# Third attention: branch counts folded into a bias table, a weight stream and the convolution's mean moved inside it, the last gate built beside the routing

## The chip, the cores and the metric

One core of a Trainium2 chip runs the whole program. The metric is the device time of one execution in microseconds (us); lower is better. The core has a matrix engine (TensorE, PE in the rows, with its weight loads as PEld), VectorE (DVE), ScalarE (ACT), GpSimd (POOL), and SyncE (SP), which issues most of the transfers from device memory. Each engine works through its own list of instructions in order, and they wait for each other on semaphores.

## The reference, cut to what matters

Three mixing layers and a mixture of experts run on 256 tokens of width 1024. The change lies in the third layer and in what follows it:

```python
# 8 heads, 256 tokens; three causal branches: (window 128, step 1), (512, 4), (2048, 16)
s = q k^T / 8 - slope_h * (t - t')         # one bias per head
out = sum_i e^{m_i} o_i / sum_i e^{m_i} l_i    # the branches are joined by their denominators
conv = silu(layer_norm_2(depthwise_conv(a * sigmoid(b)), ln_g, ln_b))    # 512 channels
x = x + gt1 * (concat([attn, conv]) @ w_out)
h2 = rms_norm(x, g_norm2) * (1 + sc2) + sh2
x = x + gt2 * hier_moe(h2, ...)            # 32 experts, 2 for each token, all in float32
# sh2, sc2, gt2: columns 3D to 6D of  silu(c) @ w_mod + b_mod  (w_mod is 1024 x 6144)
```

A key that lies in more than one branch counts once for each branch. So the joined result is one softmax in which each exponential is multiplied by the number of branches that hold the key (0 to 3).

## The kernel before

**Weights.** All weights come as pieces of 2 MB into `ring`, six slots of 16 KB in each partition. `PLAN` (from `chunk_plan()`) is the order of the pieces; a piece is loaded when the piece six places ahead of it is used up. `PLACE[stage][c]` is the place of piece c of a stage. After the plan SP loads the experts' weights, two experts (a pair) at a time, six pieces of 2 MB for a pair: two for gate, two for up, two for down (`load_pair`, line 583). For these there are nine slots: the ring's six, and the tiles `K`, `G` and `Q`.

**The modulation.** `w_mod_2` is multiplied with silu(c) in 12 pieces of 512 columns; columns 3D to 6D are the stage `mod_b`, six pieces (0 to 5). `stream(stage, c, bank)` on PE multiplies a piece and leaves a partial row (line 743; 738 for pieces 4 and 5, the gate gt2, whose rows are 512 wide), `mod_rows` on ACT copies the row out of PSUM (line 1340), and `fold` on PE turns it into columns (line 753). The gate is spread over all partitions by two products for each half (lines 1191 and 1192), and ACT copies it to `gate_row` (line 1533).

**The third attention** (`attention("c", ...)` on PE, ACT and DVE) has 8 units: 4 pairs of heads by 2 blocks of 128 queries (block 0 has 128 keys, block 1 has 256). For each unit: PE makes the scores of two heads (line 929), DVE adds the bias (`bias_c`, two instructions, line 1903) and takes the row maximum (line 1829), ACT takes the exponential (line 1387), DVE multiplies it by the branch counts and sums it (two instructions with an accumulator, line 1843), takes the reciprocal (1846) and scales (1850), PE turns the block (942), ACT copies it to `probT` (1404), PE multiplies with v (956), DVE copies the result out (1863). The engines run up to three units apart: in step n of its loop DVE does `take_out(n - 1)`, `row_max(n + 3)`, `sums(n + 2)`; PE turns unit n, makes the scores of unit n + 3 and multiplies unit n with v. The PE streams pieces 0, 1 and 2 of `mod_b` before unit 0.

**After it**, PE does in this order: `stream` of piece 3; the mean of the convolution over its channels (`feature_sum`, four products into bank 4); `stream` 4; `fold` 3; the mean of the squares (`feature_sum`, bank 2); `stream` 5; then `c_out`, the projection (`out_proj`, line 992, 8 output tiles of 8 products), which needs the attention's half of `mixT` at first and the convolution's half (from `nm["lnc", "out"]`) later. DVE subtracts the mean (2163), ACT squares (1415) and takes the root (1419), DVE takes the reciprocal (2166) and multiplies (2169), ACT applies silu (1516). Then come the logits (line 1146), the turned rows (1156), the routing on DVE (2219 to 2246), its ranks on PE (1198 to 1200), the choice of the first pair's tokens on DVE (2272), `gather` on PE (1212), and 16 pairs of experts (`experts`, gate and up at line 1246, down at 1278, the next pair's gather at 1212, the scatter at 1224). At the end of the second layer ACT issues five small loads (lines 1465 to 1471) just before it copies the rows of `mod_a`.

Of the kernel before, what the change touches and what calls it, by code (L numbers as in the profile page):

```python
# [18 lines left out]
ALU = mybir.AluOpType  # L19
# [31 lines left out]
def const_layout():  # L51
    at, n = {}, 0
    for name, w in (("ident", P), ("fold", 3), ("eps", 2), ("mean", P), ("before", P), ("dist", 2 * S),
                    ("mult", 2 * S), ("col", GRID_W), ("slot", CAP), ("desc", NE),
                    ("cos", S), ("sin", S), ("rot", P), ("band", 2 * P)):
        at[name] = (n, n + w)
        n += w
    return at, n


def constants():
    at, n = const_layout()
    out = np.zeros((P, n), np.float32)
# [25 lines left out]
    put("dist", np.where(mult > 0, d, BIG))  # L89
    put("mult", mult)  # L90
# [20 lines left out]
def chunk_plan():  # L111

    plan = []
    for stage, src, l, columns in (
# [8 lines left out]
            ("mod_b", "w_mod_2", 0, range(6, 12)), ("c_out", "w_out_2", 0, range(2))):  # L123
# [104 lines left out]
def build(nc, IN, consts_dram, relpad, out):  # L228
    CA, CN = const_layout()
    with ExitStack() as ctx:  # L230
# [40 lines left out]
        def vc(name, j=0):  # L271
# [64 lines left out]
                       "mod_b": U[:, 2048:3584].rearrange("p (b n) -> p b n", b=3)}  # L336
# [5 lines left out]
        def modrow(stage, c):  # L342

            if c < EARLY.get(stage, 0):
                return rows_beside[stage][:, c, 0:P]
# [13 lines left out]
        gate_row = cst[:, CA["dist"][0]:CA["dist"][0] + D]  # L359
# [8 lines left out]
        TURN = (6, 7, 4, 3)  # L368

# [92 lines left out]
        late_tables = cst[:, CA["dist"][0]:CA["mult"][1]]  # L462
# [73 lines left out]
        def _(sp):  # L536
# [16 lines left out]
            for n, (stage, src, l, c) in enumerate(PLAN):  # L553
                if n - SLOTS == PLACE["b_in"][5]:
                    sp.wait_ge(st["b_in"], used["b_in"][5])
                    load_bias(range(4))
                    sp.dma_start(late_tables, consts_dram[:, CA["dist"][0]:CA["mult"][1]]).then_inc(table_in, 16)
# [12 lines left out]
                if n == 5:  # L570
                    sp.dma_start(flat[:, 0:CN - CR], consts_dram[:, CR:CN]).then_inc(table_in, 16)
                    for c0, c1 in ((CF, CA["dist"][0]), (CA["mult"][1], CR)):
# [19 lines left out]
            load_pair(0, 0, after_plan, parts=range(4))  # L592
# [7 lines left out]
            load_pair(0, 0, after_plan, parts=(4, 5))  # L600
# [96 lines left out]
        def _(pe):  # L697
# [221 lines left out]
            def attention(L, q_of, k_of, v_of, stage, v0, nv):  # L919
# [18 lines left out]
                for n, (p, kind, qb, kts) in enumerate(un):  # L938
# [20 lines left out]
                    last.then_inc(at["pv"], 1)  # L959

# [22 lines left out]
            def out_proj(stage, src, width, late=KT, after=None):  # L983
# [13 lines left out]
                if late < KT:  # L997
                    for m in range(4):
                        part(m, range(late))
                    pe.wait_ge(nm["lnc", "out"], 4)  # L1000
# [7 lines left out]
            def feature_sum(bank, mat, src, n, width, ready, done):  # L1008

                for j in range(n):  # L1010
                    pe.wait_ge(ready, j + 1)
                    last = mm(ps[:, bank, 0:width], mat, src[:, j, 0:width], start=(j == 0), stop=(j == n - 1))
# [112 lines left out]
            pe.wait_ge(mod_ok, 6)  # L1125
            attention("c", lambda h, kind, qb: qTc[half(h), h // 2, qb * P:(qb + 1) * P],
# [1259 lines left out]
```

## Time and profile before

| | us |
|---|---|
| median of 3 runs | 1213.71 |
| lowest and highest | 1211.02, 1214.12 |
| the profiled execution, its own time | 1209.34 |
| the profiled execution, its span | 1207.3 |
| PE busy | 1152.9 (95%) |
| DVE busy | 544.6 (45%) |
| ACT busy | 295.7 (24%) |
| first expert product | 740.76 |

The span is the time from the first to the last recorded instruction. Busy time is what an engine's records cover. PEclk is the TensorE clock that was granted, as a share of full speed. The DMA share is the mean busy share of the core's 16 transfer engines. Times of rows are counted from the start of the span.

### The profile page before, as it was taken

How to read it: one execution, taken by the hardware profiler on the slowest of the kernel's cores; microseconds unless marked ns; L12 is line 12 of the kernel's file. 1: busy time of each engine (PE TensorE's matmuls, PEld its weight loads, DVE VectorE, ACT ScalarE, POOL GpSimd, SP SyncE). 2: the span in 40 equal slices, each digit the busy share in tenths (PEclk: the TensorE clock that was granted, in tenths of full speed). 3: DMA queues.
4: the chain of work that ended last, by engine and by line, in shares of the span. 5: the costliest groups of instructions: out<-in, count | busy, mean ns of one | idle time of the engine just before them, and what ended most of it. 6: DMA issues, size and time to landing. Idle time of an engine off the chain costs nothing.

```text
span 1207.3 us, 17553 instructions
## 1 busy us (share of the span) xinstructions
PE 1152.9 (95%) x7148; PEld 743.0 (62%) x7148; DVE 544.6 (45%) x1278; ACT 295.7 (24%) x705; POOL 22.7 (2%) x33
## 2 busy tenths in 40 slices
PE   4999999989999999999998998999999999999996
PEld 3486876668778888668885585444444444444442
DVE  3353339986575430872799623122222222222223
ACT  0000128850340001660612413111111111111112
POOL 0000000000000001110000000000000000000000
PEclk9999999999999999999999798999999999999999
DMA  9852128023442226566376695999999999999990
GB/s 344 318 209 73 68 93 326 1 75 136 140 178 101 70 70 183 124 188 211 140 279 228 246 301 202 428 427 428 426 429 428 427 429 429 427 428 430 427 413 39
DMA packets 82335, 311.54 MB, mean 258 GB/s; under 512 B 18130, under 2 KB 19229, under 8 KB 69467
## 3 DMA queue, kind: packets, MB, share of 16 engines
q1 hardware_dynamic: 78672, 309.56, 65.9%
q10 hardware_dynamic: 3386, 0.86, 0.3%
q8 instruction: 48, 0.79, 0.3%
q0 software_dynamic: 208, 0.17, 0.1%
q14 instruction: 21, 0.16, 0.0%
HBM read 309.40 MB, written 1.18 MB: 257 GB/s over the span
## 4 chain that ended last, share of the span: by engine, by line
PE 81%; DVE 12%; ACT 2%; DMA 2%; issue 1%; SPq 1%; ACTq 0%; DVEq 0%
PE ps L1246 18%; PE ps L891 17%; PE ps L1278 9%; PE ps L1212 5%; PE ps L992 5%; PE ps L1224 5%; DVE G L2146 4%; PE ps L956 2%; PE ps L942 2%; PE ps L840 2%; PE ps L1096 2%; PE ps L1072 2%; PE ps L929 2%; PE ps L743 2%; DMA ring<-in_a_w_in 2%; DVE soft L1824 1%
## 5 line engine op out<-in xcount | busy, mean ns | idle before, releaser
L1246 PE MATMUL ps<-ring,prob 128*64 128x512 f32 x704 | 188.1, 593 | 1.2 <-issue 1.2
L1246 PEld LDWEIGHTS ps<-ring,prob 128*64 128x64 f32 x704 | 61.9, 137 | 100.3 <-issue 100.3
L2311 DVE TENSOR_TENSOR prob<-ps,prob 128x512 f32<-128x512 f32 x16 | 17.2, 1075 | 193.7 <-PE ps L1246 193.7
L1278 PE MATMUL ps<-ring,prob 128*64 128x512 f32 x352 | 78.0, 596 | 0.0
L891 PE MATMUL ps<-U,ring 128*128 128x256 f32 x304 | 69.9, 381 | 1.6 <-DVE Q L1991 1.3
L1246 PE MATMUL ps<-K,prob 128*64 128x512 f32 x160 | 70.3, 592 | 0.0
L1212 PEld LDWEIGHTS ps<-bias,U 128*128 128x128 f32 x512 | 60.5, 198 | 13.4 <-issue 13.4
L1387 ACT ACTIVATE prob<-ps,soft 128x512 f32<-128x512 f32 (+2 forms) x112 | 64.1, 591 | 11.0 <-DVE soft L1829 9.0
L2319 DVE TENSOR_TENSOR probT<-ps,cst 128x512 f32<-128x512 f32 x32 | 22.1, 691 | 94.6 <-PE ps L1278 94.6
L1212 PE MATMUL ps<-bias,U 128*128 128x128 f32 x512 | 63.5, 284 | 1.1 <-DVE bias L2272 1.1
L891 PEld LDWEIGHTS ps<-U,ring 128*128 128x128 f32 x304 | 57.6, 190 | 9.9 <-DVE Q L1991 1.7
L1224 PE MATMUL ps<-probT,bias 128*128 128x512 f32 x128 | 57.9, 594 | 0.0
L1551 ACT ACTIVATE prob<-ps 128x512 f32<-128x512 f32 x16 | 9.6, 597 | 192.4 <-PE ps L1246 192.4
L1404 ACT ACTIVATE probT<-ps 128x512 f32<-128x512 f32 (+1 forms) x88 | 48.2, 585 | 34.4 <-PE ps L942 33.6
L992 PE MATMUL ps<-U,ring 128*128 128x256 f32 x256 | 56.4, 381 | 0.0
L1544 ACT ACTIVATE prob<-ps,H 128x128 f32<-128x128 f32 x64 | 24.0, 456 | 128.3 <-PE ps L1212 128.3
L942 PE MATMUL ps<-cst,prob 128*128 128x128 f32 x344 | 51.6, 288 | 2.4 <-DVE prob L1850 2.4
L992 PEld LDWEIGHTS ps<-U,ring 128*128 128x128 f32 x256 | 48.4, 190 | 7.1 <-issue 0.8
L1278 PEld LDWEIGHTS ps<-ring,prob 128*64 128x64 f32 x352 | 24.3, 137 | 45.8 <-issue 45.8
L929 PE MATMUL ps<-K,Q 64*128 64x512 f32 (+1 forms) x192 | 46.9, 568 | 1.9 <-ACT G L1375 1.3
L2296 DVE TENSOR_TENSOR U<-ps,U 128x512 f32<-128x512 f32 x64 | 44.2, 691 | 8.9 <-PE ps L1224 8.9
L2146 DVE SCALAR_TENSOR_TENSOR G<-G,conv_taps 128x256 f32<-128x256 f32 x120 | 47.7, 478 | 0.0
(378 smaller groups left out, 1839.2 us busy)
## 6 DMA issues: line engine op xcount, KB each, us to landing
ring<-in_w_exp_gate SPq DMA_DIRECT2D x22, 2048.0 KB, 18.2
ring<-in_w_exp_up SPq DMA_DIRECT2D x20, 2048.0 KB, 16.7
ring<-in_w_exp_down SPq DMA_DIRECT2D x20, 2048.0 KB, 19.9
ring<-in_w_ada SPq DMA_DIRECT2D x12, 2048.0 KB, 16.4
ring<-in_w_mod SPq DMA_DIRECT2D x12, 2048.0 KB, 8.8
ring<-in_b_w_in SPq DMA_DIRECT2D x8, 2048.0 KB, 9.0
ring<-in_a_w_in SPq DMA_DIRECT2D x5, 2048.0 KB, 17.7
ring<-in_w_in SPq DMA_DIRECT2D x5, 2048.0 KB, 9.2
```

The lines of the kernel that those rows point to most:

```text
L891: last = mm(ps[:, bank, 0:256], still[:, k, f * P:(f + 1) * P], moving[:, k, :], start=(k == 0), stop=(k == 3))
L929: last = mm(ps[:, 2 * (n % 2) + x, 0:len(kts) * P], q_of(h, kind, qb), k_of(h, kts), start=True, stop=True)
L942: last = tr(ps[:, 4 + i // 2, (i % 2) * S + x * P:(i % 2) * S + (x + 1) * P], prob[:, n % AHEAD, x * T + i * P:x * T + (i + 1) * P], ident)
L992: last = mm(ps[:, m % 4, 0:width], slot(n)[:, k, (m % 4) * P:(m % 4 + 1) * P], src[:, k, 0:width], start=(k == 0), stop=(k == KT - 1))
L1212: last = mm(ps[:, j // 4, (j % 4) * P:(j % 4 + 1) * P], h2rows[:, t, j * P:(j + 1) * P], pick[:, t, :], start=(t == 0), stop=(t == 1))
L1224: mm(ps[:, ACC_BANK[i], :], wpickT[:, t * P:(t + 1) * P], yrows[:, c * 512:(c + 1) * 512], start=True, stop=True).then_inc(scat, 1)
L1246: last = mm(ps[x * CAP:(x + 1) * CAP, 2 + i, :], xg[:, k, x * CAP:(x + 1) * CAP], chunk(n, 2 * i + x, turn)[0][:, k, :], start=(k == 0), s ...
L1278: last = mm(ps[x * CAP:(x + 1) * CAP, 5 + c, :], hidT[:, k, x * CAP:(x + 1) * CAP], chunk(n, 4 + x, turn)[0][:, k, c * 512:(c + 1) * 512], ...
L1387: last = a(prob[:, n % AHEAD, x * T:x * T + w], ps[:, 2 * (n % 2) + x, 0:w], ACT.Exp, bias=s[:, 1, x:x + 1], accum_out=None if L == "c" el ...
L1404: a(probT[:, i * S:i * S + w], ps[:, 4 + i // 2, 0:w], ACT.Copy).then_inc(at["copied"], 1)
L2146: ins = v.scalar_tensor_tensor(convo[:, j, :], glu[:, j, k:k + S], conv_taps[:, j, k:k + 1], convo[:, j, :], ALU.mult, ALU.add)
L2296: v.tensor_tensor(y, ps[:, b, :], y, ALU.add).then_inc(acc_ok, 1)
```

## The change

- Branch counts: the tables `dist` and `mult` go. A table for each head holds `log(count) - slope * distance`, or -1e30 where no branch has the key. `bias_c` adds it to both heads' scores in one instruction. ACT's exponential now makes the sum itself, and DVE's multiplication by counts goes. The table is 1.5 MB (`alibi`, in `Q`) and is loaded from ACT's queue, ahead of its copy of the row of `mod_a` piece 5; the 0.5 MB of `dist` and `mult` on SP's queue are no longer loaded.
- `mod_b` piece 3 is streamed after unit 1 of the attention. After unit 3, once DVE has taken unit 2 out, PE folds it and makes the convolution's mean (bank 5). DVE subtracts it (`center_conv`) after `sums(7)`.
- After the attention PE starts `c_out` at once; the mean of the squares is made after its first part.
- Pieces 4 and 5 are streamed after the last turned rows; `c_out` changes places with them in `PLAN`, and the loads of the first pair's up and down weights change places with them too. The gate's first half is spread after the ranks and before the first gather, its second half between the first gather and the totals.
- The load of the gate's bias row (`brow`, 4 KB) moves from the end of the attention to the five small loads of the second layer, as a sixth.
- DVE's preparation of the router's weights (`gains`, `wsum`) moves ahead of the convolution's reciprocal.

```diff
             ("c_in", "w_in_2", 0, (4, 3, 0, 1, 2)),
-            ("mod_b", "w_mod_2", 0, range(6, 12)), ("c_out", "w_out_2", 0, range(2))):
+            ("mod_b", "w_mod_2", 0, range(6, 10)), ("c_out", "w_out_2", 0, range(2)),
+            ("mod_b", "w_mod_2", 0, (10, 11))):
...
-                    sp.dma_start(late_tables, consts_dram[:, CA["dist"][0]:CA["mult"][1]]).then_inc(table_in, 16)
...
-            load_pair(0, 0, after_plan, parts=range(4))
+            load_pair(0, 0, after_plan, parts=range(2))
...
-            load_pair(0, 0, after_plan, parts=(4, 5))
+            load_pair(0, 0, after_plan, parts=range(2, 6))
...
                     last.then_inc(at["pv"], 1)
+                    if beside_unit:
+                        beside_unit(n)
...
+            def beside_c_unit(n):
+
+                if n == 1:
+                    stream("mod_b", 3, 5)
+                if n == 3:
+                    pe.wait_ge(at["o"], past["c", "o"] + 3)
+                    fold("mod_b", 3, 2, 1, 6)
+                    feature_sum(conv_mean, meanm, convo, 4, conv_ok, nm["lnc", "mean"])
+
+            def conv_variance(m):
+
+                if m == 0:
+                    feature_sum(ps[:, 5, 0:S], meanm, csq, 4, nm["lnc", "sq"], nm["lnc", "var"])
...
-            pe.wait_ge(at["o"], past["c", "o"] + len(UN["c"]) - 1)
-            stream("mod_b", 3, 5)
-            pe.wait_ge(conv_ok, 4)
-            feature_sum(4, meanm, convo, 4, S, conv_ok, nm["lnc", "mean"])
-            stream("mod_b", 4, 3)
-            pe.wait_ge(mod_ok, 7)
-            fold("mod_b", 3, 2, 1, 6)
-            feature_sum(2, meanm, csq, 4, S, nm["lnc", "sq"], nm["lnc", "var"])
-            stream("mod_b", 5, 5)
...
-            pe.wait_ge(nm["lnc", "std"], 1)
...
             turn_h(3)
-            for i, c in enumerate((4, 5)):
+            stream("mod_b", 4, 0)
+            stream("mod_b", 5, 1)
+
+            def spread_gate(i):
+
+                c = 4 + i
                 pe.wait_ge(row_ok, CHUNKS["mod_b"] + c + 1)
-                mm(ps[:, 1 + i, :], foldw, modrow("mod_b", c), start=True, stop=False)
...
             mm(ps[:, 5, NE:2 * NE], ones, sel[:, 0, :], start=False, stop=True).then_inc(ranks, 1)
+            spread_gate(0)
...
                 gather(r * PAIRS)
                 if r == 0:
+                    pe.wait_ge(h_row, 1)
+                    spread_gate(1)
                     totals()
...
                         last = a(prob[:, n % AHEAD, x * T:x * T + w], ps[:, 2 * (n % 2) + x, 0:w], ACT.Exp,
-                                 bias=s[:, 1, x:x + 1], accum_out=None if L == "c" else s[:, 2, x:x + 1])
+                                 bias=s[:, 1, x:x + 1], accum_out=s[:, 2, x:x + 1])
...
+                    if L == "c" and n == 3:
+                        mod_rows(stage, (3,), (5,))
...
+            act.dma_start(brow, IN["b_mod_2"][0:1, 5 * D:6 * D]).then_inc(rt_in, 16)
             mod_rows("mod_a", range(2, 4), (4, 5))
...
+            act.wait_ge(sig_ok, 4)
+            act.dma_start(alibi, consts_dram[:, CN:CN + NH2 // 2 * ALIBI]).then_inc(table_in, 16)
             mod_rows("mod_a", (5,), (6,))
...
-                    if L == "c":
-                        qb = un[n][2]
-                        mult = cs("mult")[:, qb * S:qb * S + w]
-                        for x in range(2):
-                            pr = prob[:, n % AHEAD, x * T:x * T + w]
-                            step(v.scalar_tensor_tensor(pr, pr, 1.0, mult, ALU.mult, ALU.mult,
-                                                        accum_out=s[:, 2, x:x + 1]))
-                        settle()
...
+                    if L == "c" and n + 3 == len(un):
+                        center_conv()
                 take_out(len(un) - 1)
+
+            def center_conv():
+                dve.wait_ge(nm["lnc", "mean"], 1)
+                dve.wait_ge(conv_ok, 4)
+                for j in range(4):
+                    v.scalar_tensor_tensor(convo[:, j, :], conv_mean, -float(D // HID), convo[:, j, :], ALU.mult, ALU.add
+                                           ).then_inc(nm["lnc", "cent"], 1)
...
-                for x in range(2):
-                    slope = 2.0 ** (-8.0 * (2 * p + x + 1) / NH2)
-                    sc = ps[:, 2 * (n % 2) + x, 0:w]
-                    step(v.scalar_tensor_tensor(sc, cs("dist")[:, qb * S:qb * S + w], -slope, sc,
-                                                ALU.mult, ALU.add))
+                sc = ps[:, 2 * (n % 2):2 * (n % 2) + 2, 0:w]
+                term = alibi[:, p * ALIBI + qb * 2 * P:p * ALIBI + qb * 2 * P + 2 * w].rearrange("p (x k) -> p x k", x=2)
+                step(v.tensor_tensor(sc, sc, term, ALU.add))
                 settle()
```

On ACT the copies of the rows of pieces 4 and 5 now stand after the turned rows and around the routing's first exponential, `take_gate(0)` after the four copies to `yacc`, and `take_gate(1)` after the first `take_gather`. The dummy root that fetches ACT's table for the convolution's root stands right after the squares.

## Rows read from the trace of the kernel before

**Rows 1.** Busy time by stretch, TensorE clock, DMA share and GB/s.

```profile
core 0: us, PE busy (x) PEld busy (x) DVE busy (x) ACT busy (x) POOL busy (x), PEclk, DMA share, GB/s
...
680.30:691.30 11.00, 11.00 (x116) 6.76 (x115) 3.35 (x8) 3.94 (x8) 0.00 (x0) 0.87 0.63 230
...
767.00:1181.00 414.00, 414.00 (x2054) 180.07 (x2050) 102.98 (x185) 60.40 (x112) 0.00 (x0) 1.00 1.00 423
```

**Rows 2.** The chain that ended last, from the third attention to the projection.

```profile
658.81 0.43 DVE prob L1843 x4
...
660.81 0.70 DVE prob L1843 x4
...
680.32 3.25 PE ps L743 x64
683.57 1.93 PE ps L1012 x8
...
691.35 17.47 PE ps L992 x80
```

**Rows 3.** The same view as rows 1, for three short stretches.

```profile
662.70:672.80 10.10, 10.05 (x52) 5.63 (x50) 9.69 (x43) 4.45 (x12) 0.00 (x0) 0.50 1.03 406
676.40:683.00 6.60, 5.61 (x68) 4.35 (x72) 1.54 (x7) 0.63 (x2) 0.00 (x0) 0.50 0.00 1
731.00:737.60 6.60, 5.50 (x26) 5.40 (x26) 0.84 (x3) 1.99 (x6) 0.00 (x0) 0.50 0.49 209
```

**Rows 4.** PE in order of time: start, duration, line, operands.

```profile
605.84 1.95 PE L743 MATMUL ps<-ring,sil 128*32 128x128 f32 x64
...
660.37 0.70 PE L929 MATMUL ps<-K 64*128 64x256 f32 x4
...
687.27 0.39 PE L753 MATMUL ps<-cst,prob 128*128 128x4 f32 x2
...
725.63 1.02 PE L1191 MATMUL ps<-prob,H 128*128 128x512 f32 x2
...
733.25 5.93 PE L1212 MATMUL ps<-bias,U 128*128 128x128 f32 x32 [1.09 <-DVE bias L2272]
...
739.17 0.39 PE L1205 MATMUL ps<-probT,H 128*128 128x32 f32 x2
740.76 13.95 PE L1246 MATMUL ps<-ring,prob 128*64 128x512 f32 x64 [1.21 <-issue]
754.65 3.84 PE L1212 MATMUL ps<-bias,U 128*128 128x128 f32 x32
```

**Rows 5.** DVE in order of time, convolution's normalisation.

```profile
690.17 1.75 DVE L2166 RECIPROCAL prob<-prob 128x256 f32<-128x256 f32 x1 [2.75 <-ACT prob L1419]
691.96 1.43 DVE L2169 TENSOR_TENSOR G<-G,prob 128x256 f32<-128x256 f32 x4
```

**Rows 6.** ACT and its queue in order of time, after the attention.

```profile
680.68 0.25 ACTq L1508 DMA_DIRECT2D cst<-in_b_mod  x1
...
686.45 1.42 ACT L1415 ACTIVATE G<-G 128x256 f32<-128x256 f32 x4 [2.53 <-DVE G L2163]
...
689.67 0.47 ACT L1419 ACTIVATE prob<-ps,cst 128x256 f32<-128x256 f32 x1
...
693.33 2.07 ACT L1516 ACTIVATE U<-G,vec 128x256 f32<-128x256 f32 x4
```

**Rows 7.** All engines in order of time, at the second layer's end.

```profile
540.82 2.17 ACTq L1470 DMA_DIRECT2D bias<-in_b_router_group  x1
...
543.30 1.56 ACTq L1471 DMA_DIRECT2D bias<-in_b_router_expert  x1
544.90 0.45 ACT L1340 ACTIVATE prob<-ps 128x128 f32<-128x128 f32 x2 [4.63 <-PE ps L743]
```

**Rows 8.** SP's issues late in the expert stage, in order of time.

```profile
1117.47 0.33 SPq L583 DMA_DIRECT2D K<-in_w_exp_up  x1
```

**Rows 9.** The same issue: size, and us from issue to landing.

```profile
K<-in_w_exp_up SPq DMA_DIRECT2D x1, 2048.0 KB, 21.7
```

**Rows 10.** PE's first product that reads that piece.

```profile
1145.87 0.59 PE L1246 MATMUL ps<-K,prob 128*64 128x512 f32 x1
```

More of the change, by code:

```diff
@@ L52, in const_layout @@
     at, n = {}, 0
-    for name, w in (("ident", P), ("fold", 3), ("eps", 2), ("mean", P), ("before", P), ("dist", 2 * S),
-                    ("mult", 2 * S), ("col", GRID_W), ("slot", CAP), ("desc", NE),
+    for name, w in (("ident", P), ("fold", 3), ("eps", 2), ("mean", P), ("before", P), ("late", D),
+                    ("col", GRID_W), ("slot", CAP), ("desc", NE),
                     ("cos", S), ("sin", S), ("rot", P), ("band", 2 * P)):
@@ L88, in constants @@
     mult = np.where(d >= 0, (d <= 128) * 1.0 + (d % 4 == 0) + (d % 16 == 0), 0.0)
-    put("dist", np.where(mult > 0, d, BIG))
-    put("mult", mult)
+    for h in range(NH2):
+        slope = 2.0 ** (-8.0 * (h + 1) / NH2)
+        term = np.where(mult > 0, np.log(np.maximum(mult, 1.0)) - slope * d, -BIG)
+        for qb in range(2):
+            w = (qb + 1) * P
+            c0 = n + h // 2 * ALIBI + qb * 2 * P + h % 2 * w
+            out[:, c0:c0 + w] = term[:, qb, 0:w]
     qc, kc = np.arange(P)[:, None] % GRID_W, np.arange(GRID_W)[None, :]
@@ L981, in _, with out_proj @@
             attention("a", q_a, k_a, v_a, "ada1", 0, 2)
-            def out_proj(stage, src, width, late=KT, after=None):
+            def out_proj(stage, src, width, late=KT, between=None, after=None):
                 def part(m, ks):
@@ L1173, in beside_c @@
                     token_logits(m - 2)
-            out_proj("c_out", mixT, S, late=4, after=beside_c)
+            out_proj("c_out", mixT, S, late=4, between=conv_variance, after=beside_c)
             token_logits(KT - 2)
@@ L1336, in mod_rows @@
                     act.wait_ge(st[stage], c + 1)
-                    if c >= 2 + EARLY.get(stage, 0):
+                    if 2 + EARLY.get(stage, 0) <= c and not spread(stage, c):
                         act.wait_ge(col_done, CHUNKS[stage] + c - 1)
@@ L2179, in _ @@
                 settle()
+            dve.wait_ge(nm["lnc", "std"], 1)
+            step(v.reciprocal(rstd[:, 0:S], rstd[:, 0:S]))
+            settle()
+            for j in range(4):
+                v.tensor_tensor(convo[:, j, :], convo[:, j, :], rstd[:, 0:S], ALU.mult).then_inc(acc2_ok, 1)
             for k in range(KT):
```

70 lines of the change are left out of this document (33 added, 37 removed).

## The prediction

> **What bounds the kernel now.** I read the view by stretch first [rows 1]. In the expert stage, from 767 us on, PE is busy without a gap (414.00 of 414.00 us) at full clock, so that whatever brings the first expert product (740.76) forward brings the end forward, as long as the weights follow. The DMA share there is also 1.00, a warning that is taken up below. Next comes the chain of work that ended last [rows 2]: through the third attention it runs over DVE (the counts' multiplication, line 1843, is on it), then over PE alone from 680.32: a stream, a feature sum, and so on to `c_out` at 691.35. In that stretch PE has no idle time at all [rows 1]. [...] So the change is worth what it moves the first expert product, and this sum is made from 656.5, where the attention starts, to 740.76.
>
> **The attention.** DVE loses line 1843 in all 8 units: 0.43 us on the chain for a unit with 128 keys, 0.70 for one with 256 [rows 2], so 4 x 1.13 = 4.5 us. The two bias instructions become one over the same elements; 0.02 us a unit at best, 0.2 in all. ACT gets an accumulator for each exponential: the nearest row is no row of this stage, so I bound it between 0 and 0.2 us an exponential; two for each unit, and DVE puts a `row_max` of about 1 us between the exponential and its use, which hides it. Without that cover it would be on the path with up to 0.4 x 8 = 3.2 us.
>
> What is added: after unit 1 PE has 1.95 us more (stream 3 at full clock [rows 4]). PE is only some 0.5 us ahead of what DVE wants next (the scores of unit 5, which stand behind the stream and the turning of unit 2), so about 1.4 us of it become a wait of DVE. After unit 3 come the fold, 0.39 [rows 4], and the mean, 1.93 [rows 2], together 2.3; behind them stand the turning of unit 4 and the scores of unit 7 (0.70 [rows 4]). Of this another 1.4 to 1.5 us reach DVE, since it still has `row_max(6)` and `sums(5)` (1.6 us) to do. `center_conv`, 4 instructions of the size of line 2169 (1.43 [rows 5]), delays `take_out(5)`, and PE's last product with v waits for that: 1.5 us more on DVE, of which about 0.9 shows at the end, as the end of the attention had waits of its own. Balance: -4.7 + 1.4 + 1.45 + 0.9 = -0.95; and the slow stretch cost the old attention about 1.0 us beyond DVE's work. So at full clock PE ends it at 680.3 - 2.0 = 678.3 and `c_out` starts at 678.5 after the last copy.
>
> **From there to the ranks.** `c_out` started at 691.35 [rows 2], now 678.5: -12.85 us. Into it comes the mean of the squares, 1.83 to 1.93: +1.85. Is the convolution ready in time? Squares follow the centering, 1.42 us [rows 6], done at 678.7, before PE has finished the first part (8 products' records of 0.218, that is 17.47/80 [rows 2]: 1.75 us). The sum ends at 682.1; root 0.47, reciprocal 1.75, first product 0.4, then four silu in 2.07 [rows 5, 6]: 686.9 with hand-offs. PE reaches the second halves at 682.1 + 3 x 1.75 = 687.4. So no wait, but with only half a microsecond to spare. The 8 instructions for the router's weights that now stand ahead of the reciprocal on DVE need about 2.5 us after 678.4 and end before the root. Streams 4 and 5 (under 2 us each) take the place of the four spread products in the shadow of DVE's routing: nothing. If that cover were gone they would cost 3.8.
>
> **Beside the first gather.** The first half of the gate (1.02 [rows 4] for one product, two products, 2.1 us) stands between the ranks and the gather, which waited 1.09 us for DVE [rows 4]: +1.0. The second half, 2.1 us, stands between the gather and the first expert product, where PE idled 1.21 [rows 4]: +0.9. The old gather lost 5.93 - 3.84 = 2.1 to the clock: -2.1 if it now runs at full clock.
>
> **The second layer.** ACT's last small loads already stand on the path: the copy of the rows follows the fifth directly, at 544.90 [rows 7]. A sixth costs 0.25 us by the same load in a quiet queue [rows 6] or up to 2.17 by its neighbours there [rows 7]. It is a single row of 4 KB, not 128 small ones, so nearer the low end: +0.6. [...] The issue of the 1.5 MB table stands ahead of ACT's copy of piece 5's row, for which ACT waits anyway until PE's stream that begins at 605.84 is over [rows 4], and the table is wanted at 656.5: nothing. Without this cover it would cost an issue, 0.25 to 2.17 again.
>
> **Sum at full clock**: -12.85 + 1.85 + 1.0 + 0.9 - 2.1 + 0.6 = -10.6 us.
>
> **The clock.** All this work is denser than before, and a slow stretch on it costs half its length, where in the old attention it was mostly hidden behind DVE. The old stretches were 10.2, 6.7 and 6.7 us long. I take one of the shorter kind on packed work: +3.4. So -7.2 us: span 1200.1, the profiled execution 1202.1, and from the median of the runs, 1213.71, which is 4.4 above the profiled execution: 1206.5.
>
> **Do the weights follow?** In the expert stage they land at 423 GB/s [rows 1], less than PE would eat, so that the lead shrinks. Late in it a piece is issued at 1117.47 and lands 21.7 us later, at 1139.2 [rows 8, 9]. PE's first record that reads it is at 1145.87 [rows 10]. The lead is 6.7 us. The stream's pace starts with the first slots that experts free, and so moves forward with PE. The last four pieces for the nine slots are now issued from the end of `c_out` on; at 2.1 MB and 423 GB/s that is 5.0 us a piece, 20 us. `c_out` ends 3 to 4 us before the spread products of 725.63 [rows 4], and the first slot was freed at half of 13.95 us after 740.76 [rows 4], 25 us after the end of `c_out`. So they are done about 5 us before. So the lead stays.
>
> **Rivals.** (A) As above, a slow stretch or two on packed work: gain 3.6 to 9.5 us, chance 0.60. (B) The clock stays full from 656 on: gain 10.6, 1203.1 us; denser work speaks for it, the lull of the routing against it. Chance 0.15. [...] (C) The work is hosted, but nothing is won: PE's queue is in order, and each thing put into the attention delays the scores DVE waits for. With slow stretches there as long as before (17 us, all now on packed work, +8.5) the gain is 2.1, 1211.6 us. Chance 0.18. (D) Slower: the slow clock holds through attention, first parts of `c_out` and both halves of the gate. Each microsecond costs 0.5; from 21 us on the gain is gone, from 28 us on it is slower by over 3.6 us; at 30 us it would be 1218. The 23.3 us of before show that such a sum is near, the dense `c_out` without any slow record speaks against it. Chance 0.07. (E) The weight stream does not move with PE: then 6.7 us is the most that can be won, 1207.0; this falls into A's figures.
>
> Changes within 0.3% (3.6 us) can't be told from none here. Faster by more: A and B, 0.75; within: C, 0.18; slower: D, 0.07. The range leaves out half of B's lower side and D: 1202.0 to 1212.5.
>
> **What would show it.** In the new profile: no multiplication with an accumulator on DVE in the attention; two waits of DVE on the scores of units 5 and 7 of 1 to 2 us each; the attention's end near 678 to 682; `c_out` directly behind, without a wait for the convolution; the first gather 1 us after its choice is made; the first expert product at 730 to 737; the expert stage still without PE idle and 466 us long. The prediction is wrong if PE waits for silu inside `c_out`, if the waits in the attention are 3 us and more, or if the first pair's up or down weights are late.

## The result, and the profile after

| | before | after |
|---|---|---|
| median, us | 1212.74 (4 runs) | 1198.82 (4 runs) |
| lowest and highest | 1211.02, 1214.12 | 1197.44, 1200.00 |
| the profiled execution: own time, span | 1209.34, 1207.3 | 1197.66, 1195.8 |
| first expert product | 740.76 | 731.75 |
| end of the last scatter product | 1196.5 | 1187.5 |

The ratio is 0.9892 [0.9879, 0.9905]: faster by 13.9 us at the medians, where the prediction said 7.2, and below its range, which ended at 1202.0. The first expert product came 9.0 us forward. From it to the last scatter product both kernels take the same 455.8 us. The rest of the gain lies behind the experts (2.5 us) and in the difference between a profiled execution and a median one: between the two profiled executions the gain is 11.7 us.

The chain that ended last, from the attention to the first gather of after, answers to [rows 2]:

```profile
663.76 1.89 PE ps L755 x64
665.64 0.37 PE ps L954 x2
666.01 0.63 PE ps L941 x4
...
669.35 1.83 PE ps L1027 x8
671.40 0.66 PE ps L941 x4
672.08 0.71 DVE ps L1938
...
677.17 0.67 PE ps L968 x8
678.21 1.99 PE ps L1006 x8
680.20 1.73 PE ps L1027 x8
681.93 15.62 PE ps L1006 x72
```

The hosted stream (L755) and the convolution's mean (the first L1027) are now on the chain, each with the scores of a later unit behind it (L941), and DVE adds the bias to these (L1938). `c_out` (L1006) starts at 678.21 directly behind the last product with v. The mean of the squares (the second L1027) stands after its first part, and then 72 products run as one: no wait for silu.

DVE of after in order of time, the two scores that it waits for:

```profile
666.69 0.70 DVE L1938 TENSOR_TENSOR ps<-ps,Q 128x512 f32<-128x512 f32 x1 [1.68 <-PE ps L941]
...
672.08 0.70 DVE L1938 TENSOR_TENSOR ps<-ps,Q 128x512 f32<-128x512 f32 x1 [1.46 <-PE ps L941]
```

PE of after in order of time, from the ranks to the first expert product, as in [rows 4]:

```profile
719.50 0.41 PE L1221 MATMUL ps<-probT,cst 128*128 128x32 f32 x2 [1.40 <-DVE probT L2269]
...
720.19 1.75 PE L1214 MATMUL ps<-prob,H 128*128 128x512 f32 x2
721.86 2.07 PE L1215 MATMUL ps<-cst,H 1*128 1x512 f32 x2
723.87 5.48 PE L1236 MATMUL ps<-bias,U 128*128 128x128 f32 x32
729.18 1.02 PE L1214 MATMUL ps<-prob,H 128*128 128x512 f32 x2
730.14 1.12 PE L1215 MATMUL ps<-cst,H 1*128 1x512 f32 x2
...
731.75 2.80 PE L1270 MATMUL ps<-ring,prob 128*64 128x512 f32 x12
```

Both halves of the gate (L1214, L1215) fill what had been two waits of PE. The first half took 3.8 us and the gather 5.48, the second half 2.1: only the first two ran at the slow clock. (At full clock the same gather takes 3.84, in `unhosted` below.) The view by stretch has the columns of [rows 1]; its first line answers to [rows 3], its second to [rows 1]:

```profile
720.50:727.30 6.80, 6.80 (x20) 3.93 (x19) 0.74 (x3) 1.19 (x4) 0.00 (x0) 0.50 0.99 410
762.00:1176.00 414.00, 414.00 (x2048) 180.42 (x2045) 105.40 (x185) 61.07 (x113) 0.00 (x0) 1.00 0.99 419
```

That is the only slow stretch between 600 us and the end of the experts; before had three there, 23.3 us together. (Both kernels also end at the slow clock, 5.3 and 4.3 us long, when PE has no work left.) PE is again without a gap through the expert stage.

**The tail.** The chain's last part, which the prediction does not mention. Before, and then after:

```profile
1197.47 0.07 DVEq L2341
1197.54 3.08 issue
1200.61 0.02 DVEq L2347
```

```profile
1188.46 0.06 DVEq L2365
1188.53 0.54 issue
1189.07 0.02 DVEq L2371
```

DVEq L2341 (L2365 in after) is DVE's branch past the further passes over the experts, which no execution here needs. From it to its next instruction DVE took 3.1 us before and 0.6 after: 2.5 us of the gain, in a place that no part of the change touches. "issue" in these rows is time in which the engine waited for nothing that the profile shows.

### The profile page after: what moved, and what is told of

Same layout as the page of the kernel before. It is cut to its first block, busy times and chain, and to the rows that moved or that the text cites. A ratio compares the mean times of both kernels' runs of the same rounds, so it can differ in the third digit from the quotient of the medians.

```text
span 1195.8 us, 17528 instructions
## 1 busy us (share of the span) xinstructions
PE 1145.7 (96%) x7148; PEld 735.3 (61%) x7148; DVE 540.7 (45%) x1236; ACT 297.2 (25%) x722; POOL 22.8 (2%) x33
## 4 chain that ended last, share of the span: by engine, by line
PE 83%; DVE 12%; DMA 2%; ACT 2%; issue 1%; SPq 1%; DVEq 0%; ACTq 0%
PE ps L1270 18%; PE ps L903 17%; PE ps L1303 9%; PE ps L1236 5%; PE ps L1006 5%; PE ps L1248 5%; DVE G L2180 4%; PE ps L968 2%; PE ps L941 2%; PE ps L852 2%; PE ps L1111 2%; PE ps L1087 2%; PE ps L954 2%; PE ps L755 2%; DMA ring<-in_a_w_in 2%; DVE soft L1859 1%
## 5 line engine op out<-in xcount | busy, mean ns | idle before, releaser
L1006 PE MATMUL ps<-U,ring 128*128 128x256 f32 x256 | 56.7, 381 | 0.4 <-DVE U L1890 0.4
L1006 PEld LDWEIGHTS ps<-U,ring 128*128 128x128 f32 x256 | 48.2, 190 | 7.1 <-DVE U L1890 0.6
L941 PE MATMUL ps<-K,Q 64*128 64x512 f32 (+1 forms) x192 | 46.8, 568 | 1.9 <-ACT G L1402 1.3
```

The costliest lines, as they stand in the source:

```text
L941: last = mm(ps[:, 2 * (n % 2) + x, 0:len(kts) * P], q_of(h, kind, qb), k_of(h, kts), start=True, stop=True)
L1006: last = mm(ps[:, m % 4, 0:width], slot(n)[:, k, (m % 4) * P:(m % 4 + 1) * P], src[:, k, 0:width], start=(k == 0), stop=(k == KT - 1))
```

## The experiments

Three questions were open: which part of the change brings the 9.0 us; whether the 2.5 us of the tail come with one of its parts, or only from where the branch stands in DVE's code (the change takes 41 instructions out ahead of it); and whether the clock is better because the attention is filled, because of the multiplications' removal, or by chance. The start of the third attention differs by up to 4.7 us between the profiled executions (657.0 to 661.7), so profiles are compared from the attention's first row maximum on. Slow stretches near 30 and 345 us are part of that: with 3.4 us of them it starts at 657.0 and 657.1, with 6.8 at 657.8 to 660.0, with 10.2 at 658.7 to 661.7. "To the expert" is the time from there to the first expert product: 83.76 before, 74.62 after. Medians are given with the ratio to before, whose executions were timed beside each kernel's on the same chip. The mean granted clock of an execution is given as a share of full speed.

### The counts alone, the hosting undone, the gate ahead, padding of 41

`counts_alone` is before with the new table, the exponentials' own sums and no multiplication:

```diff
-                step(v.scalar_tensor_tensor(pr, pr, 1.0, mult, ALU.mult, ALU.mult,
-                                            accum_out=s[:, 2, x:x + 1]))
...
+                step(v.tensor_tensor(sc, sc, term, ALU.add))
```

> The kernel before with one part of the change: the per-head bias table, the exponential that makes its own sum, and no multiplication by counts on DVE. Theory 1 (DVE's work bounds the attention): DVE loses 4 x (0.43 + 0.70) = 4.5 us, c_out starts at 691.35 - 4.5 = about 687, and the first expert product moves from 740.8 to about 736. Rival (PE bounds the attention while its clock is at 0.50): c_out starts at 689 to 691. Theory 2 (the 2.5 us of the end come from where DVE's instructions lie in memory, since the changed kernel runs 41 DVE instructions fewer): DVE's step between the branch after the last pair and the last semaphore wait falls from 3.1 to about 0.5 us here too, since 40 of the 41 are gone in this kernel; if it stays at 3.1, the number of instructions before it is not what decides, or 40 is not enough.

Measured: 1205.64 (1200.04 to 1211.03, 10 runs), 0.9954 [0.9933, 0.9976]. Its profile has 84.42 us to the expert. The first profile of before has 83.76 with 17 us of slow clock in the attention; a second one (`before_again`, below), with the same 23.9 us as here, has 85.18. So at like clock 0.8 us of the expected 4.5 are won before the experts. The tail brings another 2.5: the step after the branch takes 0.59 us. What is left of the median's 5.6 us lies in executions whose clock held better than this one's (it had 0.983). The view by stretch shows why so little is won here:

```profile
660.90:684.80 23.90, 21.73 (x141) 13.78 (x142) 12.81 (x42) 9.34 (x37) 0.00 (x0) 0.50 0.58 226
```

Almost the whole attention ran at 0.50, and there PE, busy 21.73 of 23.90 us, is the bound, as the rival had it: DVE waited 4.1 us for scores in it, in the first profile of before not at all. A lighter DVE is worth little then. The timed executions bear it out: the mean clock and the span go together, from 0.991 and 1198.2 us to 0.981 to 0.983 and 1206.6 to 1209.2. The execution at 0.991 was as quick as two of after's four (1198.2, at 0.991 and 0.992).

`unhosted` is after, with the stream, the fold, the mean and the centering right behind the attention:

```diff
-                      ... vcr[:, kt, h * HD:(h + 1) * HD], "mod_b", 2, 1, beside_c_unit)
+                      ... vcr[:, kt, h * HD:(h + 1) * HD], "mod_b", 2, 1)
+            stream("mod_b", 3, 5)
+            fold("mod_b", 3, 2, 1, 6)
+            feature_sum(conv_mean, meanm, convo, 4, conv_ok, nm["lnc", "mean"])
```

> The changed kernel with stream 3, its fold, the convolution's mean (in bank 4) and the centering taken out of the attention and put right behind it. Theory 1 (hosting only trades PE time behind the attention, 4.3 us, against DVE waits of 1.7 and 1.5 us and 0.7 us of centering inside it): the attention ends 3.5 to 4.5 us earlier, at about 673.5, c_out starts at about 678, a wait of 1 us for the squares appears before the mean of squares, and the whole is 0.5 to 1.5 us slower than the changed kernel. Rival (hosting is what brings the gain): c_out starts 4 us later, at 682, and the whole is 4 us slower. If the attention, emptier of PE work, falls to clock 0.50, it is 2 to 4 us slower in either case, and the clock of the stretch 656 to 680 says so.

Measured: 1198.71 (1196.24 to 1204.50, 4 runs), 0.9907 [0.9872, 0.9942]; 75.78 to the expert. `c_out` starts 25.35 us after the first row maximum, against 21.08 in after, but with 10.2 us of slow clock in the attention where after had none. Its routing shows what the gate costs without slow clock:

```profile
725.92 1.10 PE L1217 MATMUL ps<-prob,H 128*128 128x512 f32 x2
726.95 1.12 PE L1218 MATMUL ps<-cst,H 1*128 1x512 f32 x2
728.00 3.84 PE L1239 MATMUL ps<-bias,U 128*128 128x128 f32 x32
```

From the ranks to the expert it takes 9.02 us, against 12.25 in after: the slow stretch on packed work cost after 3.2 us. `c_out` came 4.3 us later, as the rival said, but with a slow stretch in the attention that after didn't have, and the routing gave 3.2 of it back. Hosting is worth 1.2 us in these profiles and 1.8 by the ratios, less than the intervals can tell from nothing.

`gate_ahead` is after, with pieces 4 and 5 streamed between attention and `c_out` and both halves of the gate spread before the ranks:

```diff
+            stream("mod_b", 4, 4)
+            stream("mod_b", 5, 7)
...
-            stream("mod_b", 4, 0)
-            stream("mod_b", 5, 1)
...
+            spread_gate(0)
+            spread_gate(1)
```

> The changed kernel with streams 4 and 5 put back between the attention and c_out, and both spread products of the gate back before the ranks, with the old order of loads. By the sum: two streams of 1.85 on the path, +3.7; the two halves of the gate no longer beside the first gather, -2.0 at full clock and more at 0.50: 1.7 us slower than the changed kernel at full clock, about equal where the changed kernel's spread products and gather run at 0.50 and these don't. Rival (the gate's place costs nothing beside the routing): 3.7 us slower.

Measured: 1202.36 (1202.23 to 1204.47, 4 runs), 0.9937 [0.9920, 0.9954]; 76.57 to the expert, 1.95 more than after. Its PE, in order of time:

```profile
682.22 3.64 PE L749 MATMUL ps<-ring,sil 128*32 128x512 f32 x32 [0.38 <-DVE U L1888]
...
729.66 5.33 PE L1237 MATMUL ps<-bias,U 128*128 128x128 f32 x32 [1.10 <-DVE bias L2294]
...
736.57 0.65 PE L1271 MATMUL ps<-ring,prob 128*64 128x512 f32 x2 [1.21 <-issue]
```

The streams' 3.6 us are back on the path, and the old waits of 1.10 and 1.21 us are there again. Moving the gate beside the routing is a part that pays: 1.95 us in the profiles, about what the sum gave it (3.6 out, 1.9 in), and 5.4 by the ratios (0.9937 against 0.9892), more than the expected 1.7. The two profiles differ in their clock (this one had 3.4 us of slow clock in the attention and 6.8 on the ranks and the gather), so the 1.95 is not the gate's alone.

`after_pad41` adds waits that are long fulfilled to DVE's part ahead of the branch:

```diff
                 if r == 0:
+                    for _ in range(41):
+                        dve.wait_ge(cst_in, 16)
                     dve.wait_ge(perm_in, 32)
```

> The changed kernel with 41 waits on an already fulfilled semaphore put into DVE's program where DVE idles before the first gather is taken. They put DVE's branch after the last pair back to about the place in its program that it has before the change. Theory 2 (place in memory): DVE's step from that branch to its last semaphore wait is back at about 3.1 us instead of 0.6, and the whole is 2.5 us slower. Rival (it hangs on the state of the transfer queues or of other engines at that moment): it stays at 0.6 and the time is the changed kernel's within 0.1%.

Measured: 1200.45 (1198.18 to 1201.00, 4 runs), 0.9910 [0.9893, 0.9926]. The step after the branch stayed at 0.6 us. But 41 waits became only 20 instructions: the trace counts 1610 of DVE, against 1590 in after and 1631 in before. So this did not test the intended place of the branch. What it shows is the clock: with a slow stretch of 6.8 us in the attention and another on the gather it takes 77.18 to the expert, `c_out` starting 23.64 after the first row maximum, against 74.62 and 21.08 in after. This slow stretch in the hosted attention cost 2.6 us.

### Before once more and padded, the attention filled, the gate early

`before_again` is before, unchanged.

> The kernel before, unchanged, profiled once more. After the last pair DVE took 3.1 us from its branch to its next instruction in the first profile; in the changed kernel and in all four variants run so far it took 0.6. If the 3.1 belongs to this program (theory 2a), it is 3.1 again. If it is chance of that one execution (theory 2b), it is 0.6 here, and nothing of the change's gain may be put down to it.

Measured: a span of 1210.5 us, 85.18 to the expert, and 3.13 us from the branch to the next instruction: the step is a trait of the kernel, not of one execution. The slow clock lay 23.9 us long over the attention, not 10.2 and 6.7 as in the first profile of before, whose own time, 1209.34, was below the lowest of the runs timed beside it.

`before_pad41` has the same padding in before.

> The kernel before with 41 waits on an already fulfilled semaphore in DVE's program, in the idle stretch before the first gather is taken. If the 3.1 us belong to the place of DVE's branch in its program (theory 2a), 41 instructions more move it and the step should be 0.6; if it is chance (2b), it is 0.6 in both kernels of this call.

Measured: a span of 1212.1 us, and a step of 2.94 us at 1651 instructions. The 0.6 us that was expected did not come, as the padding was 20 instructions here too and not 41. The slow clock lay over the attention for 27.3 us.

`counts_filled` is `counts_alone` with a product that nobody uses after each unit of the attention:

```diff
+                    if L == "c":
+                        mm(ps[:, 5, 0:S], ident, qTc[:, 0, :], start=True, stop=True)
```

> The kernel counts_alone with one product more on PE behind each unit of the attention (identity times 256 columns of q, into the unused bank 5, read by nobody): 8 products of about 0.45 us at full clock. Theory 3 (what the change wins in the attention, it wins by keeping PE's clock up; alone, the lighter DVE work is eaten by PE at clock 0.50): the stretch 657 to 680 runs mostly at full clock, it is 16 to 19 us from the first row maximum to PE's last product with v instead of 24.5, and the median is 2 to 6 us below counts_alone although PE does more. Rival (the clock is lost for another reason than sparse work, such as the phase of the execution): the clock is at 0.50 for as long as in counts_alone, and the time is 1 to 3 us longer than there.

Measured: 1205.93 (1203.30 to 1207.79, 9 runs), 0.9955 [0.9941, 0.9969]; 81.34 to the expert. The slow stretch in the attention shrank from 23.9 to 6.8 us in the profile, and the mean clock of the timed executions was 0.989 to 0.993, against 0.981 to 0.991 without the products. The median did not move. The filled attention kept more of the clock, and the filler, 8 products of 0.54 us at full clock in an engine that the next scores wait for, cost as much as the clock gave back: at the same mean clock (0.990 and 0.991) its executions took 5.5 us longer than those of `counts_alone` (median spans of 1205.9 and 1203.8 against 1200.4 and 1198.2). The profile looks better than the median (3.1 us less to the expert than `counts_alone`), and its attention started 2.4 us later. In this pair of kernels a fuller attention goes with less slow clock, and the filler was too dear for what it brought. But slow stretches ran on with hardly a gap in PE's records too, 6.80 of 6.80 us in after and 10.05 of 10.10 in before [rows 3].

`spread_early` is after with the gate's first half ahead of the wait for the choice that the ranks need:

```diff
+            spread_gate(0)
             pe.wait_ge(sel_ok, 1)
...
-            spread_gate(0)
```

> The changed kernel with the gate's first half spread before the ranks, in the time in which PE waits for the routing (1.4 us idle), instead of behind them. By the sum: ranks 0.7 us later, the first gather then at ranks + 2.6 us instead of + 4.4: 1.1 us faster at full clock. If the clock falls because of the lull in the routing, filling it keeps the gather at full clock in more executions, and it is 2 to 4 us faster. Rival: no difference, since the clock falls anyway and the ranks come later.

Measured: 1199.03 (1193.89 to 1201.31, 6 runs), 0.9898 [0.9875, 0.9921]; 75.55 to the expert, with slow clock for 6.8 us in the attention and 3.4 in the first gather. Not to be told from after.

### The padding at the right length, the lull filled, the multiplications put back

The branch is 41 instructions nearer in after. By the count of 41 waits as 20 instructions, 82 waits make 41 and 174 waits 87. If the place of the branch decides (theory 2a), after with the 41 should have a step near before's 3.1 us; if something else of the change does, it stays at 0.6. That 87 instructions forward would do for before what 41 back had done was the author's estimate; no run ahead of it shows it.

> The changed kernel with 82 waits on a fulfilled semaphore in DVE's idle stretch; two of them become one instruction (41 gave 20 more in the trace), so DVE's branch after the last pair now stands 41 instructions later, exactly where it stands before the change. [...]

> The kernel before with 174 such waits, 87 instructions. [...] Theory 2a: the step behind DVE's branch is 0.6 us instead of 3.1. Rival: 3.1 as in the two profiles of before.

Measured for `after_pad82`: 1201.38 (1200.44 to 1203.66, 4 runs), 0.9907 [0.9883, 0.9931]; 74.62 to the expert, the same as after to the hundredth. The chain's last part:

```profile
1192.30 0.07 DVEq L2367
1192.36 2.79 issue
1195.15 0.02 DVEq L2373
```

For `before_pad174` (span 1211.3; the padding itself delays the first expert product by 2.2 us):

```profile
1204.00 0.06 DVEq L2343
1204.06 0.54 issue
1204.60 0.02 DVEq L2349
```

The step is 2.85 us in `after_pad82` and 0.60 in `before_pad174`, as theory 2a and that estimate had it. So the stall can be given to after and taken from before, with no work changed:

| kernel | DVE instructions | us from the branch to the next |
|---|---|---|
| after | 1590 | 0.60 |
| `counts_alone` | 1591 | 0.59 |
| `after_pad41` | 1610 | 0.58 |
| `after_mult` | 1622 | 0.60 |
| before, `before_again` | 1631 | 3.14, 3.13 |
| `after_pad82` | 1631 | 2.85 |
| `before_pad41` | 1651 | 2.94 |
| `before_pad174` | 1718 | 0.60 |

What the time goes to can be looked for in the transfers. The view of the queues (packets, MB, share of 16 engines) gives two packets of instructions for before from 1197.5 to 1200.6, the slow step:

```profile
q8 instruction: 1, 0.02, 1.9%
q14 instruction: 1, 0.01, 0.6%
```

The slow step of `after_pad82`, from 1192.3 to 1195.2, has the same two:

```profile
q8 instruction: 1, 0.02, 3.1%
q14 instruction: 1, 0.01, 1.0%
```

After has them too, in a stretch of the same length behind its branch, 1188.5 to 1191.6:

```profile
q8 instruction: 1, 0.02, 2.5%
q14 instruction: 1, 0.01, 1.0%
```

What differs is their place. In after the q14 packet stands at 1189.6, 0.6 us behind DVE's next instruction. Each of the fourteen profiles has such a packet, 0.6 to 0.7 us behind that instruction. The four profiles with the slow step (before, `before_again`, `before_pad41`, `after_pad82`) have one q14 packet more, 1.0 to 1.3 us behind the branch, in the slow step itself (1198.8 in before); none of the quick ones has. The author's guess is a wait for instructions that are not there yet when the branch has jumped over the code of the passes that aren't run. No run shows what the packet holds or that DVE waits for it; this is argued from the packet's place alone. What the padding shows is that the place of the code decides: 2.85 us against after's 0.60, and 0.60 against before's 3.14.

`lull_filled` is after with a product that nobody uses, put ahead of PE's wait for the choice that the ranks need:

```diff
+            pe.wait_ge(row_ok, CHUNKS["mod_b"] + 5)
+            mm(ps[:, 2, :], foldw, modrow("mod_b", 4), start=True, stop=True)
             pe.wait_ge(sel_ok, 1)
```

> The changed kernel with one more product of 512 columns on PE (about 1.0 us at full clock) in the 1.4 us in which it waits for the routing; its result is read by nobody. Theory 3 (sparse work on PE lowers the clock): the slow stretch at the ranks and the first gather becomes rarer or shorter, and where it is gone the first expert product comes 3.3 us earlier relative to the start of c_out; the median is 0 to 3 us below the changed kernel. Rival (the lull is too short to matter, or the slow stretch comes from the thin products of the logits before it): the slow stretch stays as it was, 6.8 us, and the time too.

Measured: 1197.97 (1194.50 to 1201.45, 4 runs), 0.9879 [0.9845, 0.9914]; 73.96 to the expert. The routing and the gather ran at full clock, 9.01 us from the ranks to the expert and 3.84 for the gather:

```profile
661.60:668.50 6.90, 6.90 (x48) 4.71 (x50) 4.94 (x17) 3.18 (x15) 0.00 (x0) 0.51 1.05 386
716.00:731.00 15.00, 14.56 (x102) 8.88 (x101) 6.46 (x32) 9.71 (x20) 0.00 (x0) 1.00 0.95 362
```

But this execution had its slow stretch in the attention instead (first line), and the median's gain over after lies within the intervals. It is the lowest median of the study; that it beats after is not shown. Nor is it shown that the product kept the routing's clock: in `unhosted`, without it, only the first 3.4 us, over a stream, were slow.

`after_mult` is after with DVE's pass over the exponentials put back (its result, the sum apart, is what it reads, so it costs the time and changes nothing):

```diff
+                        for x in range(2):
+                            pr = prob[:, n % AHEAD, x * T:x * T + w]
+                            step(v.scalar_tensor_tensor(pr, pr, 1.0, pr, ALU.mult, ALU.max,
+                                                        accum_out=s[:, 2, x:x + 1]))
```

> The changed kernel with two DVE instructions put back into each unit of the attention, of the shape and with the accumulator of the old multiplication by counts (they multiply by 1 and leave the values as they are): the rest of the change without its lighter DVE work. By the sum DVE has 4.5 us more, of which the waits of 1.7 and 1.5 us behind the hosted work take up some 1.5 to 2: the attention ends 2.5 to 3 us later than in the changed kernel, and the whole is that much slower. Rival (the counts' removal is off the path once PE hosts the stream and the mean): within 1 us of the changed kernel. Second rival (nothing is taken up): 4.5 us slower.

Measured: 1206.14 (1200.96 to 1207.57, 7 runs), 0.9943 [0.9922, 0.9963]; 79.06 to the expert. That is 4.4 more than after, but 1.9 more than `after_pad41`, whose two slow stretches lie in the same places. At the slow clock DVE waits for PE anyway, and these waits take up part of the passes' 4.5 us. DVE's waits for scores in the attention (us in total, times, longest), in `after_pad41` and then here, are 2.8 us shorter with the passes:

```profile
DVE ps L1938 <- PE ps L941: 5.6, 4, 2.3
```

```profile
DVE ps L1944 <- PE ps L941: 2.8, 3, 1.4
```

By the ratios the passes cost 6.2 us (0.9943 against 0.9892), more than any of the expectations: with them the timed executions also had a lower clock, 0.986 to 0.991, against 0.991 to 0.994. Alone the counts' removal brought 5.6 us at the median, and 2.5 of those were the branch. That leaves 3.1, against 6.2 in the changed kernel; with these intervals it is not shown that the removal pays more there.

**The parts side by side.** In the profiles, to the expert, after's 9.1 us over before stand against 4.4 for the counts' removal, 1.95 for the gate's place and 1.2 for hosting, each with a clock pattern of its own. By the ratios the same three are 6.2, 5.4 and 1.8 us, and the branch is 2.5. These add up to more than after's 13, so that they are not independent, or the few executions of each drew different clocks. What is shown is that the counts' removal and the gate's place each bring something, and that for hosting a gain is not shown.

## Why the prediction was right and wrong

**Right, by its own steps** (what was predicted stands in brackets). DVE has two waits, of 1.68 and 1.46 us (1.4 and 1.45, on the scores of units 5 and 7). `c_out` starts at 678.21 (678.5), directly behind the attention, and doesn't wait for the convolution. From its start to the ranks it takes 41.29 us, against 39.48 before: +1.81 for the mean of the squares (+1.85). For the second half of the gate, it takes 2.40 us from the gather's end to the expert in `unhosted` and 1.57 before: +0.83 (+0.9). Where the gather had the full clock it took 3.84 us, 2.1 less than before (-2.1). One slow stretch of 6.8 us fell on packed work and cost 3.2 (6.7 us, 3.4). That it was one, and of this length, was a guess that came true: `after_pad41` and `after_mult`, whose work there is the same or nearly so, had two. The experts' products take as long as before and have no idle time, and the weights followed.

**Too dear in the sum, 1.8 us.** The first half of the gate was priced at +1.0. From the ranks to the gather it took 2.50 us before and takes 2.78 in `unhosted`, +0.3, so that 0.7 were too much. Some 0.5 of that is clock: before, the rank products lay in the slow stretch too (0.61 for the second pair against 0.39), and with them at full clock `before_pad41` needs 1.96. `c_out`, with the small load ahead of it, started 13.1 us earlier, where the sum had 12.85 - 0.6: that is 0.8. The rest is 0.2 of the slow stretch and 0.1 of rounding. The load was priced at 0.6 from rows of 0.25 and 2.17. ACT of after, in order of time:

```profile
541.41 1.92 ACTq L1499 DMA_DIRECT2D bias<-in_b_router_group  x1
543.64 0.36 ACTq L1500 DMA_DIRECT2D bias<-in_b_router_expert  x1
544.03 0.40 ACTq L1501 DMA_DIRECT2D cst<-in_b_mod  x1
544.48 0.28 ACT L1367 ACTIVATE prob<-ps 128x128 f32<-128x128 f32 x1 [3.62 <-PE ps L755]
```

It took 0.40, and as the load ahead of it took 0.36 where [rows 7] have 1.56, the copy of the rows began even earlier than before (544.48 against 544.90). The third attention's first row maximum came at 657.13, against 657.00 before, so that little of the 0.6 was paid.

The starts of neighbouring small loads took from 0.36 us (above) to 2.17 [rows 7]; the trace has no landing time for them, so how a start compares with its transfer is not shown.

**The step that failed: "whatever brings the first expert product (740.76) forward brings the end forward", taken to mean that nothing behind it can move by itself.** The experts' products obeyed. But [rows 1] end at 1181, [rows 2] end at the projection, and the sum has no term for anything behind the experts; it put this part at nothing without a reason. Its own sign, "the expert stage still without PE idle and 466 us long", failed there: from the first expert product to the end of the span it took 464.0 us. Read to the chain's end, the sum would have had its row of 3.08 us of "issue" behind a branch as a doubtful term, which an edit that shifts DVE's code may remove or bring. It was worth 2.5 us, shown by padding in both directions, and it came from no part of the change's design: that it fell on the good side was luck.

**The second: the base.** The sum was made in one profiled execution and taken off a median 4.4 us above it ("from the median of the runs, 1213.71"), as if the changed kernel stood as far above its own. After's profiled execution, 1197.66, is 1.2 below its median: 3.2 us. Part of the 4.4 was the draw of three executions: in the later experiments before took 1211.3 at the median of 39. Part goes with the clock: of these 39, the 11 at 0.980 to 0.982 took about 1213, the 7 at 0.986, the clock of the first profile, 1208.9. So a median execution of before had more to give back than the profiled one: 13.9 us between the medians, 11.7 between the profiled executions, of which 9.0 is the first expert product's and 2.5 the branch's. By the ratio's interval the gain is 11.5 to 14.7.

The count closes: from the predicted 1206.5 to the measured 1198.8 it is 7.7 us, of which 1.8 were too dear in the sum, 2.5 the branch and 3.2 the base, with 0.2 of rounding and of time outside the span. Without the branch the median would have been about 1201.3, still below the range's 1202.0. The mechanism in front of the experts was right; what failed were the term behind them and the base.

**The rivals.** C, slow stretches as long as before, now on packed work, is excluded for after: its four executions had a mean clock of 0.991 to 0.994, which at (1 - clock) / 0.5 of 1197 us is 14 to 22 us at 0.50 over the whole span. In the profiled one 4.3 of them lie at the end and 3.4 near 345 us, and if that holds for the others too, at most 14 are left for all the rest. The 39 later executions of before had 0.980 to 0.989, or 27 to 48 us. B, the full clock from 656 us on, did not happen in after; variants came near it: the lowest executions of `spread_early` and `lull_filled` had a mean clock of 0.997 and spans of 1192.1 and 1192.7. D, slower, is excluded by the interval, and so is E: the product moved 9.0 us, more than the lead of 6.7, and the weights were not late.

**What stays open.** It is open why the attention of after and its variants is less often slow. Removing the multiplications doesn't do it by itself (23.9 us slow in `counts_alone`), and filling seems to do part (6.8 in `counts_filled`), but `unhosted`, whose attention is filled no more than that of `counts_alone`, had 10.2, and executions between 0.985 and 0.995. One profile of each, and so few executions, don't separate the hosting from luck. That DVE waits for a packet of instructions in the slow step fits the place of these packets in all fourteen profiles, but no run shows the wait itself.

## What to carry to other kernels

Read the chain of the profile to its last row before summing a change up: a step of several microseconds of "issue" behind a branch, with nothing but packets of instructions moving in it, may belong to the place of the code and not to the work. Here padding of 41 instructions ahead of it switched it on (0.60 us in after, 2.85 in `after_pad82`). Take the base and the change from more than one profiled execution, or at least look whether the one at hand has the clock of a median one. Where two engines are near to each other and one of them has two clock levels (0.50 and full here), relief of the other can be worth little at the lower level: of the counts' 4.5 us, 0.8 reached the path in `counts_alone`, with 23.9 us of slow clock in the attention, and 1.9 by `after_mult`, with 6.8.

## What the hardware showed that was not expected

- A taken branch on DVE over code that isn't run cost 2.85 to 3.14 us or 0.6, by its place alone. Padding after by 41 instructions brought the slow step (2.85 us), padding before by 87 removed it (0.60). In the slow step one packet of queue q14 moved that the quick ones don't have; the packets behind it move in both.
- Added waits that are already fulfilled show as about half as many instructions: 41 as 20, 82 as 41, 174 as 87.
- 82 waits that are already fulfilled cost after nothing to the first expert product (74.62 both times); 174 cost before 2.2 us there.
- Before had 23.9 us of slow clock in its attention in one execution and 17 in another. Its third attention began at 658.7 and 657.0 us, with 10.2 and 3.4 us of slow clock near 30 and 345 us.
- With 8 unused products of 0.54 us at full clock the slow clock in the profiled attention was 6.8 us instead of 23.9, and the mean clock of the executions 0.989 to 0.993 instead of 0.981 to 0.991; the median stayed where it was.
